# Attention row blocks 0 and 1 of a head pair as one unit of 384 columns, with transposes ahead of value products

## The reference, cut to what matters

```python
for i in range(S // Q_BLOCK):                      # Q_BLOCK = 128, so i = 0..3
    q0, q1 = i * Q_BLOCK, (i + 1) * Q_BLOCK
    logits = einsum(q[q0:q1], k[:q1]) * scale + c[q0:q1, None] - c[None, :q1]
    p = softmax(where(causal, logits, -inf))
    outs.append(einsum(p, v[:q1]))
```

## Time and profile before

| What | Value |
|---|---|
| runs | 2133.42, 2134.06, 2136.66 us |
| the profiled execution: span | 2134.6 us |
| TensorE matmul busy | 2083.2 us, 98% |
| TensorE weight load busy | 1644.9 us, 77% |
| VectorE busy | 1235.0 us, 58% |
| ScalarE busy | 832.5 us, 39% |
| GpSimd busy | 206.5 us, 10% |
| share of TensorE in the chain that ended last | 88% |

### The profile page before, as it was taken

The page is one execution under the profiler, slowest core; times in us unless marked ns, Lnnn a source line. Parts: engine busy times, 40 slices in busy tenths (PEclk is TensorE's granted clock), DMA queues, the critical chain, the costliest instruction groups (busy, mean ns, idle before and its releaser), DMA issues.

```text
span 2134.6 us, 26510 instructions
## 1 busy us (share of the span) xinstructions
PE 2083.2 (98%) x10728; PEld 1644.9 (77%) x10728; DVE 1235.0 (58%) x1896; ACT 832.5 (39%) x1344; POOL 206.5 (10%) x176
## 2 busy tenths in 40 slices
PE   8999999999999999999999999999999999999998
PEld 7776887678878886666788888787777777888886
DVE  5665756446677777987544344475675755443442
ACT  5344544345323233225423223344464454232232
POOL 1321001011000004453000000100000010000001
PEclk9999999999999999999999999999999999999999
DMA  6322432124777773662233332121221232323321
GB/s 202 97 69 90 137 101 79 34 66 162 254 253 246 268 248 109 166 169 84 94 119 99 99 99 96 56 70 50 60 70 50 70 107 91 105 94 98 99 99 40
DMA packets 218554, 245.51 MB, mean 115 GB/s; under 512 B 9144, under 2 KB 203192, under 8 KB 212288
## 3 DMA queue, kind: packets, MB, share of 16 engines
q1 hardware_dynamic: 208784, 231.73, 33.2%
q10 hardware_dynamic: 9648, 12.08, 2.3%
HBM read 237.75 MB, written 3.78 MB: 113 GB/s over the span
## 4 chain that ended last, share of the span: by engine, by line
PE 88%; DVE 5%; ACT 3%; DMA 1%; issue 1%; ACTq 0%; POOL 0%; SPq 0%; DVEq 0%
PE bank L1323 24%; PE bank L1331 24%; PE bank L1327 24%; PE bank L1348 2%; PE bank L1352 2%; PE bank L1356 2%; PE bank L1457 1%; PE bank L1531 1%; PE bank L1402 1%; PE bank L1508 1%; PE bank L1415 1%; PE bank L1395 1%; PE bank L1440 1%; PE bank L1521 1%; DVE wL L1938 1%
## 5 line engine op out<-in xcount | busy, mean ns | idle before, releaser
L1323 PE MATMUL bank<-hH,wH 128*128 128x512 f32 (+1 forms) x1672 | 634.1, 396 | 18.0 <-ACT wH L1572 8.4
L1331 PE MATMUL bank<-hL,wH 128*128 128x512 f32 (+1 forms) x1672 | 616.8, 386 | 0.0
L1327 PE MATMUL bank<-hH,wL 128*128 128x512 f32 (+1 forms) x1672 | 616.4, 386 | 0.0
L1567 ACT ACTIVATE wH<-raw 128x1024 fp32r<-128x1024 f32 (+1 forms) x376 | 334.2, 939 | 355.7 <-PE bank L1331 283.9
L1938 DVE TENSOR_TENSOR wL<-raw,wH 128x1024 fp32r<-128x1024 f32 (+1 forms) x340 | 375.9, 1142 | 137.0 <-ACT wH L1567 137.0
L1323 PEld LDWEIGHTS bank<-hH,wH 128*128 128x128 f32 x1672 | 313.8, 188 | 109.5 <-issue 29.7
L1331 PEld LDWEIGHTS bank<-hL,wH 128*128 128x128 f32 x1672 | 314.2, 188 | 64.8 <-DVE hL L1958 0.9
L1327 PEld LDWEIGHTS bank<-hH,wL 128*128 128x128 f32 x1672 | 314.5, 188 | 63.6 <-issue 3.1
L1323 PE MATMUL bank<-hidH,wH 128*128 128x512 f32 x768 | 299.1, 389 | 1.9 <-ACT hidH L1729 1.9
L1331 PE MATMUL bank<-hidL,wH 128*128 128x512 f32 x768 | 298.9, 389 | 0.0
L1327 PE MATMUL bank<-hidH,wL 128*128 128x512 f32 x768 | 298.8, 389 | 0.0
(11 more groups left out here) (220 smaller groups left out, 2037.5 us busy)
## 6 DMA issues: line engine op xcount, KB each, us to landing
raw<-in_mlp SPq DMA_DIRECT2D x64, 1024.0 KB, 5.2
araw<-in_ada_w SPq DMA_DIRECT2D x48, 1024.0 KB, 5.0
raw<-in_w_ff SPq DMA_DIRECT2D x32, 1024.0 KB, 7.4
raw<-in_hgrn_in SPq DMA_DIRECT2D x32, 512.0 KB, 3.7
raw<-in_w_in SPq DMA_DIRECT2D x11, 1024.0 KB, 5.3
raw<-in_conv_in SPq DMA_DIRECT2D x16, 512.0 KB, 4.0
u<-conv_u ACTq DMA_DIRECT2D x24, 270.0 KB, 5.1
raw<-in_w_mv SPq DMA_DIRECT2D x4, 1024.0 KB, 5.1
```

Of the source, the lines that this page charges most:

```text
L1323: mm(out, wH[:, s, m:m + 128], xh[:, k, 0:width], start=k == 0, stop=False)
L1327: mm(out, wL[:, s, m:m + 128], xh[:, k, 0:width], start=False, stop=False)
L1331: i = mm(out, wH[:, s, m:m + 128], xl[:, k, 0:width], start=False, stop=k == KB - 1)
L1567: do(wH[:, s, c], raw[:, r, c], ACT.Copy).then_inc(*s_whi.up(n, x))
```

## The change

Row blocks 0 and 1 of a head pair become one unit, `rows` = (0, 1). Each of its heads holds one bank, one `Lb` and one `PTb` slot; row block 0 uses columns 0 to 127 of them and row block 1 columns 128 to 383 (`c0`). Scores, bias, maximum, exp, division and transposes remain one instruction group per head and row block; the copy of the transposes becomes one of 384 columns per head. There are 24 units in place of 32. `stagger` gets `second=True`: of the live units the second oldest now takes its step first, then the oldest, then the others. In even rounds transposes of unit n-2 therefore come ahead of value products of unit n-3, and in odd rounds the division of one unit ahead of the copy of the older one. RW goes from 1.4 to 1.87.

```diff
-RW, RM = 1.4, 0.52
+RW, RM = 1.87, 0.52
...
-def stagger(gens, gap):
+def stagger(gens, gap, second=False):
...
-        for g in list(live):
+        for g in live[1:2] + live[:1] + live[2:] if second else list(live):
             if next(g, "end") == "end":
                 live.remove(g)
...
-    def pair(self, g, p, i):
+    def pair(self, g, p, rows):
...
+        heads = [[dict(g=g, h=2 * p + x, i=i, w=128 * (i + 1), c0=128 * (i * (i + 1) - rows[0] * (rows[0] + 1)) // 2,
+                       pb=64 * x, id=(g, 2 * p + x, i), pid=id_, sc=self.chead[g, 2 * p + x]) for i in rows]
+                 for x in range(2)]
+        us = [u for both in zip(*heads) for u in both]
         wait = []
-        for u in us:
-            u["b"], free = self.lin.get()
+        for units in heads:
+            b, free = self.lin.get()
             wait += free
+            for u in units:
+                u["b"] = b
         self.do("scores", us=us, blk=blk, id=id_, after=wait)
...
+        for units in heads:
+            b, free = self.lin.get()
+            for u in units:
+                u["b2"] = b
+                self.do("turn", u=u, after=free if u is units[0] else ())
+            self.lslots.put(units[0]["l"], ("mm", "turn", units[-1]["id"]))
         yield
-        for x, u in enumerate(us):
-            u["p"], u["pfree"] = self.pslots.get()
-            self.do("turned", u=u)
-            self.lin.put(u["b2"], ("act" if x else "dve", "turned", u["id"]))
+        for x, units in enumerate(heads):
+            slot, free = self.pslots.get()
+            for u in units:
+                u["p"] = slot
+            self.do("turned", u=units[-1], pfree=free, w=sum(u["w"] for u in units))
+            self.lin.put(units[0]["b2"], ("act" if x else "dve", "turned", units[-1]["id"]))
         yield
...
-                for i in range(4):
-                    yield self.pair(g, p, i)
+                for rows in ((0, 1), (2,), (3,)):
+                    yield self.pair(g, p, rows)
...
-        alongside(stagger(self.pairs(), 2), rest(), [RW])
+        alongside(stagger(self.pairs(), 2, second=True), rest(), [RW])
...
-                    for j in range(i + 1):
-                        pe.wait_ge(*s_act.at("v", g, j, 256 * (it["us"][0]["h"] // 4)))
-                        for u in it["us"]:
-                            h, pb = u["h"], u["pb"]
-                            m = mm(banks[6 + it["o"]][pb:pb + 64, 128 * i:128 * i + 128], vt[:, g, j, 64 * h:64 * h + 64],
-                                   PTb[:, u["p"], 128 * j:128 * j + 128], start=j == 0, stop=j == i)
+                    for i in sorted({u["i"] for u in it["us"]}):
+                        for j in range(i + 1):
+                            pe.wait_ge(*s_act.at("v", g, j, 256 * (it["us"][0]["h"] // 4)))
+                            for u in it["us"]:
+                                if u["i"] != i:
+                                    continue
+                                h, pb, c = u["h"], u["pb"], u["c0"] + 128 * j
+                                m = mm(banks[6 + it["o"]][pb:pb + 64, 128 * i:128 * i + 128],
+                                       vt[:, g, j, 64 * h:64 * h + 64], PTb[:, u["p"], c:c + 128], start=j == 0, stop=j == i)
```

More of the change, by code:

```diff
@@ L376, in softmax @@
         self.do("soft_div", us=us, add=add)
-    def pair(self, g, p, i):
-        w, blk, id_ = 128 * (i + 1), 4 * g + p, (g, p, i)
-        if i == 0:
+    def pair(self, g, p, rows):
+        blk, id_ = 4 * g + p, (g, p, rows[-1])
+        if rows[0] == 0:
             self.ob[g, p] = self.obk.get()
         o, ofree = self.ob[g, p]
-        us = [dict(g=g, h=2 * p + x, i=i, w=w, pb=64 * x, id=(g, 2 * p + x, i), pid=id_, sc=self.chead[g, 2 * p + x])
-              for x in range(2)]
+        heads = [[dict(g=g, h=2 * p + x, i=i, w=128 * (i + 1), c0=128 * (i * (i + 1) - rows[0] * (rows[0] + 1)) // 2,
+                       pb=64 * x, id=(g, 2 * p + x, i), pid=id_, sc=self.chead[g, 2 * p + x]) for i in rows]
+                 for x in range(2)]
+        us = [u for both in zip(*heads) for u in both]
         wait = []
-        for u in us:
-            u["b"], free = self.lin.get()
+        for units in heads:
+            b, free = self.lin.get()
             wait += free
+            for u in units:
+                u["b"] = b
         self.do("scores", us=us, blk=blk, id=id_, after=wait)
-        for u in us:
-            u["l"], u["lfree"] = self.lslots.get()
-            self.do("bias", u=u)
+        for units in heads:
+            slot, free = self.lslots.get()
+            for u in units:
+                u["l"], u["lfree"] = slot, free
+                self.do("bias", u=u)
         yield
@@ L396, in pair @@
         next(steps)
-        for u in us:
-            self.lin.put(u["b"], ("dve", "max", u["id"]))
+        for units in heads:
+            self.lin.put(units[0]["b"], ("dve", "max", units[-1]["id"]))
         yield
@@ L401, in pair @@
         yield
[L402 to L408, removed]
-        yield
-        for x, u in enumerate(us):
-            u["p"], u["pfree"] = self.pslots.get()
-            self.do("turned", u=u)
-            self.lin.put(u["b2"], ("act" if x else "dve", "turned", u["id"]))
+        for units in heads:
+            b, free = self.lin.get()
[3 more added lines that the diff above has]
+            self.lslots.put(units[0]["l"], ("mm", "turn", units[-1]["id"]))
+        yield
+        for x, units in enumerate(heads):
+            slot, free = self.pslots.get()
+            for u in units:
+                u["p"] = slot
+            self.do("turned", u=units[-1], pfree=free, w=sum(u["w"] for u in units))
+            self.lin.put(units[0]["b2"], ("act" if x else "dve", "turned", units[-1]["id"]))
         yield
[L415 to L418, removed]
+        self.do("values", us=us, g=g, o=o, id=id_, last=[units[-1] for units in heads], ofree=ofree if rows[0] == 0 else ())
+        for units in heads:
+            self.pslots.put(units[0]["p"], ("mm", "out", id_))
+        if rows[-1] == 3:
             self.do("heads", blk=blk, o=o, id=id_)
@@ L1650, in scalar_program @@
                     if u["pb"]:
-                        for ev in u["pfree"]:
+                        for ev in it["pfree"]:
                             act.wait_ge(*event(ev))
                         act.wait_ge(*s_mm.at("turn", u["id"]))
-                        do(PTb[:, u["p"], 0:u["w"]], banks[u["b2"]][:, 0:u["w"]], ACT.Copy).then_inc(
+                        do(PTb[:, u["p"], 0:it["w"]], banks[u["b2"]][:, 0:it["w"]], ACT.Copy).then_inc(
                             *s_act.up("turned", u["id"]))
@@ L2353, in pool_program @@
                     u = it["u"]
-                    L, i, w = Lb[:, u["l"], 0:u["w"]], u["i"], u["w"]
+                    i, w = u["i"], u["w"]
+                    L = Lb[:, u["l"], u["c0"]:u["c0"] + w]
                     for ev in u["lfree"]:
```

27 lines of the change are left out of this document (15 added, 12 removed).

## The result

The changed kernel takes 2126.8 us, the median of 5 runs (2125.25 to 2128.64), against 2134.96 us for 5 runs of the kernel before: 8.2 us less, ratio 0.996 with a 95% interval of 0.995 to 0.997. The prediction was 8.6 us less. The profiled execution of the changed kernel took 2125.25 us with a span of 2123.5; a run's time is thus about 1.8 us more than its span. By the same difference the span of 2134.6 us before belongs to an execution of about 2136.4 us, an estimate, above the median of the runs and not 0.5 over it.

What follows compares the result with a forecast made beforehand. TensorE was taken to bound the kernel, its matmuls filling 98% of the span, part of it fixed cost without new columns. The terms -5.6 - 2.0 - 1.7 + 0.7 = -8.6 us gave 2125.5 us, range 2119 to 2131.

Steps and rivals of the forecast that it cites:

- The visits: TensorE's groups between linear work: eight visits fewer, each saving 0.69 us of fixed cost, 5.6 us less.
- the squares: TensorE's wait for ScalarE's copy, queued behind the squares of `mem`: 1.0 us left of 2.46, no half clock expected.
- the second place: TensorE's wait for ScalarE's copy, queued behind exps and eight copies of `mem`: 1.9 us in place of 0.6.
- The end: Stage end: 1.55 us of half steps no longer hides the last copy and square; 0.7 us more, bounds 0 and 1.55.
- The bound of 0.85 plus 0.21: Merged scores on TensorE: if each row block paid its own 0.21 us, they would take 1.06, taking back 1.7 us.
- The order: Transposes ahead of value products on TensorE: 0.10 us in each of 20 visits, 2.0 us less.
- The waits: TensorE's two waits for ScalarE's copies in the stage: 2.9 us in place of 4.6, 1.7 us less.
- At nothing: Fewer transpose copies, VectorE's division ahead of the older copy, and loads and bias order: no effect on time.
- rival 1: Both waits for ScalarE's copies disappear, covered by the doubled spacing of visits: 2122.6 us, chance 0.17.
- rival 2: Both waits stay and TensorE falls to half clock after each: 2128.6 us, chance 0.12.
- rival 3: Merged blocks each pay their fixed cost and the new order saves nothing: 2131.6 us, chance 0.08.
- rival 4: Slower: a late division holds up each visit at its first transpose; at 0.6 us a visit 2139.9 us, chance 0.03.

Runs made afterwards that it cites:

- order undone: Changed kernel with value products put back ahead of transposes, merged unit and RW 1.87 kept: 2130.4 us, ratio 0.9979.
- order alone: Changed kernel with 32 units and RW 1.4 as before, so only transposes ahead of value products is new: 2131.8 us, ratio 0.9984.
- exp first: Changed kernel with the exp of the third oldest unit also ahead of value products: 2126.0 us, ratio 0.9956.
- value products last: Changed kernel with the oldest unit stepping last, so each visit runs transposes, scores, value products: 2130.8 us, ratio 0.9976.
- end covered: Changed kernel with last rounds' counts altered to leave two half steps behind the last value products (one was left): 2127.0 us, ratio 0.9959.
- loads first: Changed kernel with the loads of `mem` ahead of pair 1's table loads in the DMA queue: 2126.3 us, ratio 0.9960.
- even rounds alone: Changed kernel with the new order in even rounds only, oldest unit first in odd rounds: 2126.4 us, ratio 0.9959.
- all together: Changed kernel with exp ahead of value products in even rounds, oldest first in odd, early `mem` loads and the end cover: 2124.0 us, ratio 0.9948.

## Why the prediction was right

**The visits.** This was the largest term, 5.6 us, and rested on nothing but the starts in the earlier trace rows. (Eight times 0.69 is 5.5, not 5.6.) With the merge alone the stage fell by 7.72 us (221.30 - 213.58). Of this 2.78 are waits and half clock: 4.88 lost before (2.52 at the squares, 1.57 by the clock, 0.79 at the second place), 2.10 in that kernel. The end became 0.84 dearer. That leaves 7.72 - 2.78 + 0.84 = 5.78 us for eight visits, 0.72 each where I had 0.69. The bound of 0.85 plus 0.21 for merged scores did not hold; they take 0.86.

**The order.** Predicted 0.10 a visit and 2.0 us, measured 0.14 and 2.8. The rows before had given 0.09 for the entry and 0.05 for the transposes; the prediction took 0.10 of these 0.14, for fear that the new neighbours would cost more. They don't: value products take 0.80 behind transposes (0.81 behind linear work) and scores 0.86 behind value products (0.85 behind transposes). The prediction's other figure, a quarter of 0.69 for one change in four, made 3.4 us; the runs lie between.

**The waits.** Predicted 2.9 us left of 4.6, measured 0.9 + 2.4 = 3.3 left of 4.9: 1.6 less where I said 1.7. The wait at the squares came as worked out, link by link. The maximum is negated 4.1 us after the end of the scores, as predicted (179.68 against 175.58), ScalarE's copy ends 15.4 us after them (191.01; predicted 15.7), and TensorE's own way takes 14.6 (predicted 14.7): 0.9 lost, 0.84 of it idle, for 1.0. (The prediction's "one visit behind the first norm, not three" holds in rounds, not in visits.)

At the second place ScalarE's queue was right and the step where TensorE meets it was not. The copy ends 9.0 us after the value products (209.04 against 200.08); the prediction's terms, 1.45 + 7.6, make the same, though it wrote 9.2 and so 1.9 us where they give 1.8. But it let value products meet that copy. In the new order the next unit's transposes stand ahead of them, and half of these need a bank that the same copy frees, so 0.48 us of transposes come behind it as well: 2.4 and not 1.8. This term the prediction left out. With the order undone value products do meet the copy directly, and the place costs 1.8. Nor had I written down that the first linear matmul behind the memory's sums needs the copies of `mem` itself; TensorE stands there for 1.2 us, but within the same delay. That the total of the waits comes out at 1.6 for 1.7 is partly luck, since the losses left out, 0.5 here and 0.3 in what the kernel before lost, cancel in part.

**The end.** Predicted 0.7 us dearer, measured 0.8: from the end of value products to the fillers it was 3.26 us with 1.55 of work in it (280.39 to 283.65), and is 2.55 without.

**At nothing.** No run tries the merged copies alone; the sum below leaves nothing for them. The claim that VectorE's new order in odd rounds costs nothing was wrong by 0.7 us, in one place.

**The sum.** -5.8 - 2.8 - 1.6 + 0.8 = -9.4, against 9.3 in the stage and 8.2 in the medians of the runs. The stage was thus predicted 0.7 us short of its gain: 0.8 by the order, 0.2 by the visits, less 0.1 each by the waits and the end. That the medians moved by 8.2, nearer to the forecast of 8.6, is no merit of it: the difference between stage and medians is within what the runs of one kernel scatter (2125.25 to 2128.64), and the 1.57 us of half clock stand in the one profile of the kernel before and need not be in its other runs.

**The rivals.** The waits did not vanish in the changed kernel (rival 1); with exp ahead of value products the one at the squares does, and the other falls to 0.9. No half clock followed either wait (rival 2). Merged blocks do not pay twice (rival 3). In the changed kernel no transpose waited for a division (rival 4): the waits name ScalarE's copies, and no line of VectorE's division.

## What to carry to other kernels

Where TensorE shows 98% busy, read the starts of successive instructions: fixed costs at changes of layout count as busy, and here merging two small groups and saving one change of layout in a visit were worth 8.6 of 9.3 us. When units interleave, write out per engine what stands ahead of each instruction in its queue: here a copy that was long ready stood behind a late division, and putting it first took 0.7 us off at no cost that the profile shows. Follow a late item to every wait that hangs on it, the buffers that it frees too: here a bank cost 0.5 us that value products did not. When work is spread by a rate, see what is left for the last round, where it hides the chain behind the last unit.

## What was not expected of the hardware

The clock fell to half in each profiled execution, at a few places that repeat, but not at all of them in each. The table of four stretches (start and end, length, then busy time of TensorE, its weight loads, VectorE, ScalarE and GpSimd, then the granted clock, the busy share of the DMA engines and the GB/s that they moved) for the last kernel:

```profile
401.00:405.00 4.00, 3.50 (x5) 1.50 (x6) 0.00 (x0) 0.89 (x2) 0.00 (x0) 0.67 0.01 4
596.00:600.00 4.00, 3.28 (x8) 2.46 (x9) 3.29 (x4) 2.53 (x4) 0.00 (x0) 0.61 1.02 380
824.00:828.00 4.00, 2.86 (x4) 1.31 (x5) 3.97 (x7) 2.30 (x4) 2.45 (x3) 0.70 0.00 2
971.00:975.00 4.00, 4.00 (x12) 3.17 (x13) 4.00 (x7) 2.73 (x5) 0.00 (x0) 0.67 0.02 4
```

and for the changed kernel:

```profile
401.00:405.00 4.00, 1.76 (x6) 0.90 (x6) 1.54 (x5) 2.25 (x7) 0.00 (x0) 0.83 0.00 0
596.00:600.00 4.00, 2.12 (x9) 1.15 (x8) 2.64 (x4) 2.21 (x4) 0.00 (x0) 1.00 0.79 274
824.00:828.00 4.00, 1.82 (x3) 0.83 (x4) 3.93 (x7) 1.75 (x4) 2.54 (x2) 0.86 0.01 2
971.00:975.00 4.00, 3.70 (x16) 3.11 (x17) 3.77 (x7) 2.81 (x5) 0.00 (x0) 1.00 0.00 0
```

A stretch's clock is its mean. Over shorter stretches a fall reads 0.50 in its middle; in the changed kernel 402 to 408 us reads 0.91, 0.50 and 0.73 by stretches of 2 us, so that this fall takes 0.18 + 1.00 + 0.54 = 1.7 us. Every other fall between 300 and 2100 us takes as much, but for one of twice that in the kernel with value products last. All kernels, with their falls in that stretch:

| Kernel | median of the runs | stage | span less stage | falls |
|---|---|---|---|---|
| before | 2134.96 | 221.30 | 1913.3 | 1 |
| changed | 2126.8 | 212.04 | 1911.5 | 2 |
| order undone | 2130.4 | 213.58 | 1915.0 | 2 |
| order alone | 2131.8 | 215.38 | 1913.9 | 2 |
| exp first | 2126.0 | 209.62 | 1914.7 | 2 |
| value products last | 2130.8 | 212.05 | 1919.0 | 4 |
| end covered | 2127.0 | 211.48 | 1910.6 | 1 |
| loads first | 2126.3 | 211.09 | 1913.0 | 1 |
| even rounds alone | 2126.4 | 211.34 | 1910.7 | 1 |
| all together | 2124.0 | 209.16 | 1916.3 | 4 |

The last kernel met half clock at all four places and spent 1916.3 us outside the stage (2125.5 - 209.2), the changed one at two and spent 1911.5. Two falls more are 3.4 of these 4.8 us; the rest is not traced. So the same code outside the stage differs by 5 us between executions, more than half of what this change brought; in the same profile the last kernel has the shorter stage and the longer span. Within the stage only the kernel before fell to half clock, behind the wait of 2.46 us; the order alone had a wait of 1.68 us without it. One case does not show that the length of the wait decides, and it was not tried.
